# Router fed with the sums ahead of the norm, and the half split of the slab after the experts given to GpSimd

## What is computed

```
proj = x @ w_in[l]                          # retention, window and latent attention follow
mix  = concat([ret_o, swa_o, mla_o]) @ w_out[l]
x    = layer_norm(ALPHA * x + mix, ln1_g[l], ln1_b[l])
scores = sigmoid(x @ router_w)              # 16 experts, one router_w for both layers
biased = scores + router_bias
# best group of 4 (sum of its two best biased scores), then the 2 best experts in it
# gates = their unbiased scores, normalised to sum 1
y    = sum over the chosen experts of down(silu(gate(x)) * up(x) * gate)
x    = layer_norm(ALPHA * x + y, ln2_g[l], ln2_b[l])
```

## Time and profile before

| | us |
|---|---|
| runs, median of 3 | 1554.58 (1554.37 to 1555.19) |
| the profiled execution | 1554.16 |
| its span | 1552.3 |

### The profile page before, as it was taken

One profiled execution on the slowest core, in us unless ns is written; L12 is line 12 of the kernel. 1 busy time (PEld: TensorE's weight loads), 2 busy tenths in 40 slices (PEclk: granted clock), 3 DMA queues, 4 the chain that ended last, 5 costly groups with the idle time before them and its releaser, 6 DMA issues.

```text
span 1552.3 us, 20392 instructions
## 1 busy us (share of the span) xinstructions
PE 1525.1 (98%) x7476; PEld 1167.2 (75%) x7476; DVE 835.7 (54%) x1126; ACT 710.5 (46%) x1179; POOL 88.8 (6%) x159
## 2 busy tenths in 40 slices
PE   8999999999999999999999999999999999999998
PEld 7886445877443788888888888878888888888886
DVE  4675215476422755546667555565555556755544
ACT  5662123674212544446474444453444537554443
POOL 2420000140000000002000000000000010000000
PEclk9999999999999999999999999999999999999999
DMA  7537997546699655566345655546555653655551
GB/s 247 204 135 296 372 421 294 173 142 279 248 421 414 220 184 192 183 207 199 115 156 170 210 191 183 186 152 208 185 185 191 208 164 109 203 190 189 189 189 56
DMA packets 165986, 328.30 MB, mean 211 GB/s; under 512 B 8874, under 2 KB 106896, under 8 KB 152992
## 3 DMA queue, kind: packets, MB, share of 16 engines
q1 hardware_dynamic: 164992, 323.52, 59.5%
q0 software_dynamic: 928, 3.89, 0.8%
HBM read 326.33 MB, written 1.05 MB: 211 GB/s over the span
## 4 chain that ended last, share of the span: by engine, by line
PE 90%; DVE 3%; DMA 3%; ACT 2%; issue 1%; DVEq 1%; POOL 0%; SPq 0%; POOLq 0%; ACTq 0%
PE bank L449 23%; PE bank L451 23%; PE bank L450 23%; PE bank L1221 6%; PE bank L1267 3%; DMA sb_raw<-w_in 2%; PE bank L853 1%; PE bank L1180 1%; PE bank L1181 1%; DMA sb_raw<-ffn_w 1%; PE bank L1275 1%; PE bank L1276 1%; DVE sb_wlo L445 1%; PE bank L930 1%; PE bank L882 1%; ACT sb_whi L438 1%
## 5 line engine op out<-in xcount | busy, mean ns | idle before, releaser
L445 DVE TENSOR_TENSOR sb_wlo<-sb_raw,sb_whi 128x1024 fp32r<-128x1024 f32 (+2 forms) x419 | 483.3, 1197 | 347.4 <-ACT sb_whi L438 347.0
L438 ACT ACTIVATE sb_whi<-sb_raw 128x1024 fp32r<-128x1024 f32 (+2 forms) x419 | 408.0, 1027 | 322.1 <-PE bank L451 303.6
L449 PE MATMUL bank<-sb_whi,sb_op_hi 128*128 128x512 f32 (+2 forms) x1216 | 475.3, 391 | 6.5 <-DVE sb_op_lo L2012 3.5
L451 PE MATMUL bank<-sb_whi,sb_op_lo 128*128 128x512 f32 (+2 forms) x1216 | 467.8, 385 | 0.0
L450 PE MATMUL bank<-sb_wlo,sb_op_hi 128*128 128x512 f32 (+2 forms) x1216 | 467.1, 384 | 0.0
L449 PEld LDWEIGHTS bank<-sb_whi,sb_op_hi 128*128 128x128 f32 x1216 | 228.7, 188 | 53.3 <-issue 4.3
L451 PEld LDWEIGHTS bank<-sb_whi,sb_op_lo 128*128 128x128 f32 x1216 | 228.6, 188 | 46.1
L450 PEld LDWEIGHTS bank<-sb_wlo,sb_op_hi 128*128 128x128 f32 x1216 | 228.9, 188 | 42.6
L449 PE MATMUL bank<-sb_whi,sb_lat_hi 128*128 128x512 f32 (+2 forms) x456 | 175.7, 385 | 1.0 <-DVE sb_wlo L445 1.0
L451 PE MATMUL bank<-sb_whi,sb_lat_lo 128*128 128x512 f32 (+2 forms) x456 | 174.5, 383 | 0.0
L450 PE MATMUL bank<-sb_wlo,sb_lat_hi 128*128 128x512 f32 (+2 forms) x456 | 174.4, 382 | 0.0
(11 more groups left out here) (269 smaller groups left out, 1337.3 us busy)
## 6 DMA issues: line engine op xcount, KB each, us to landing
sb_raw<-ffn_w SPq DMA_DIRECT2D x264, 512.0 KB, 4.3
sb_moe<-exp_w_gate_up SPq DMA_DIRECT2D x46, 1024.0 KB, 9.7
sb_raw<-w_in SPq DMA_DIRECT2D x84, 512.0 KB, 4.6
sb_moe<-exp_w_down SPq DMA_DIRECT2D x26, 1024.0 KB, 10.0
sb_raw<-w_out SPq DMA_DIRECT2D x32, 512.0 KB, 4.4
sb_per_block<-exp_w_gate_up SPq DMA_DIRECT2D x8, 1024.0 KB, 7.0
sb_xT<-exp_w_gate_up SPq DMA_DIRECT2D x6, 1024.0 KB, 10.2
sb_xg<-exp_w_gate_up SPq DMA_DIRECT2D x4, 1024.0 KB, 8.9
```

The costliest lines, as they stand in the source:

```text
L438: nc.scalar.activation(h, r, ACT.Copy).then_inc(hi_made.sem, 1)
L445: nc.vector.tensor_tensor(o, r, h.bitcast(F32), ALU.subtract).then_inc(lo_made.sem, 1)
L449: nc.tensor.matmul(ps, hi, wh, start=first, stop=False)
L451: return nc.tensor.matmul(ps, lo, wh, start=False, stop=last)
```

## The change

There are two parts.

**1. The router is fed with the sums.** The logits of a normed token are ((v − mean)·rstd·g + b)·W, which is rstd · v·W' + b·W, where W' is g·W with its column mean taken off. So the router needs no normed tokens: it takes v, the sums in the banks, and rstd comes in afterwards.

- In layer 0's set-up both layers' W' and b·W are made: GpSimd loads ln1_g and ln1_b beside other vectors (NORM1), VectorE multiplies (4 operations of 128x128) and sums (4 reductions), TensorE adds over partitions by a matmul with ones, 128x64, and VectorE takes off the mean and copies the tails b·W.
- ScalarE copies the four banks to `sums_of` (sums_out, line 1780 of the changed kernel); VectorE's bn_stats wait for these copies. TensorE transposes the sums; chunk 0's eight transposes stand inside the mix, ahead of its last quarter. All copies to xT are on ScalarE.
- VectorE makes the logits from the fold: rstd times it plus the tail (`logits`), and ScalarE's sigmoid reads them.
- The last step of chunk 1's norm goes from VectorE to ScalarE (times rstd, `scaled`) and GpSimd (plus b, two adds of 128x512). Of chunk 0's two token_lo, the second is made by GpSimd (`xs_lo0`), the first stands on VectorE between `hot` and the slot numbers.
- TensorE runs one filler instead of four; open_residual waits for `ln1` and is spread over the stage.

**2. The half split by GpSimd.** The second half of the lo split of the slab that follows the experts is made by GpSimd, between its second and third power −1/2. VectorE's part is the first half, then both last down_lo; at the layer's end it waits until GpSimd has raised `lo_made`.

```diff
@@ GpSimd @@
                 for n in range(4):
+                    if n == 2:
+                        moe_done(pool, l, last_use(WLO_SLOT[1]))
+                        pool.wait_ge(lo_made.sem, 2 * RING + 2 * slab_number(0, S1, l + 1, 1) + 1)
+                        split_lo(pool, slab_number(0, S1, l + 1, 1), 1, parts=(1,), on=nc.gpsimd)
                     pool.wait_ge(F["ln_var"].sem, F["ln_var"].after(l, n + 1))
                     nc.gpsimd.tensor_tensor(lrstd[:, n % 2:n % 2 + 1], lve[:, n % 2:n % 2 + 1], half[:, 0:1], ALU.pow).then_inc(F["ln_rstd"].sem, 1)
+                    if n == 1:
+                        for nh in range(2):
+                            v, cols_of = x[:, 1, 512 * nh:512 * nh + 512], slice(512 * nh, 512 * nh + 512)
+                            pool.wait_ge(F["normed"].sem, F["normed"].after(l, nh + 1))
+                            nc.gpsimd.tensor_tensor(v, v, table[:, 1, cols_of], ALU.add).then_inc(F["ln1"].sem, 1)
+                        pool.wait_ge(F["xs_hi"].sem, F["xs_hi"].after(l, 1))
+                        lo, hi = (t[:, 0, 4:8, :] for t in (xs_lo, xs_hi))
+                        v = x[:, 0, 512:1024].rearrange("p (q j) -> p j q", j=4)
+                        nc.gpsimd.tensor_tensor(lo, v, hi.bitcast(F32), ALU.subtract).then_inc(F["xs_lo0"].sem, 1)
@@ TensorE @@
+                if l == 0:
+                    pe.wait_ge(rw_summed.sem, 1)
+                    nc.tensor.matmul(bank[4][:, 0:2 * DEPTH * NE], c("ones"), rw_sums, start=True, stop=True).then_inc(rw_total.sem, 1)
...
                 for ch in range(NC):
                     for nh in range(2):
                         if ch == 0:
                             slab_ready(num(S1_OUT + 2 + nh))
+                        elif nh == 1:
+                            if l == 0:
+                                pe.wait_ge(rw_centred.sem, 1)
+                            routing_transposes(0)
...
-                routing_transposes(0)
+                routing_transposes(1)
                 router(0)
+                router(1)
+                fold(0)
+                fold(1)
+                wait(F, "ln1", l, 2)
                 open_residual(0)
-                routing_transposes(1)
-                fold(0)
-                router(1)
-                fold(1)
-                open_residual(1)
-                kept_busy(3, 512, const[:, 0:512])
+                wait(F, "ln1", l, 3)
+                open_residual(1, (0,))
+                kept_busy(1, 512, const[:, 0:512])
...
-                kept_busy(1, 512, const[:, 0:512], 7)
+                wait(F, "ln1", l, 4)
+                open_residual(1, (1,))
@@ ScalarE @@
+                sums_out(0, 0)
+                sums_out(0, 1)
+                sums_out(1, 0)
                 routing_out(0)
                 routing_out(1)
+                sums_out(1, 1)
+                routing_out(2)
+                routing_out(3)
                 logit_out(0)
+                logit_out(1)
...
+                wait(F, "scaled", l, 1)
+                scaled(0)
+                wait(F, "logits", l, 1)
+                nc.scalar.activation(scores, biased, ACT.Sigmoid).then_inc(F["routed"].sem, 1)
+                scaled(1)
+                wait(F, "ln1", l, 2)
                 token_hi(0)
-                routing_out(2)
-                logit_out(1)
-                wait(F, "folded", l, 2)
-                nc.scalar.activation(scores.rearrange("p c e -> p (c e)"), bank[5][:, 0:32], ACT.Sigmoid).then_inc(F["routed"].sem, 1)
+                wait(F, "ln1", l, 4)
                 token_hi(1)
@@ VectorE @@
+                def logits():
+                    dve.sem_inc(F["scaled"].sem, 1)
+                    wait(F, "folded", l, 2)
+                    for ch in range(NC):
+                        i = stt(out=biased[:, ch, :], in0=bank[5][:, NE * ch:NE * ch + NE], scalar=lrstd[:, ch:ch + 1],
+                                in1=tails[:, NE * l:NE * l + NE], op0=ALU.mult, op1=ALU.add)
+                    i.then_inc(F["logits"].sem, 1)
...
-                token_lo(0, 0)
-                token_lo(0, 1)
...
+                token_lo(0, 0)
                 wait(F, "ranked", l, 1)
...
+                    following(1, (0,))
                     for nh in range(2):
-                        following(1, (nh,))
                         down_lo(PAIRS - 1, nh)
...
+                dve.wait_ge(lo_made.sem, 2 * RING + 2 * slab_number(0, S1, l + 1, 2))
```

More of the change, by code:

```diff
@@ L396, in program @@
             ("mix_c0", 2, 0), ("ln_var", 4, 0), ("ln_rstd", 4, 0), ("ln1", 4, 0), ("table", 64, 0),
-            ("xT_a", 3, 0), ("xT_d", 1, 0), ("logit", 8, 0), ("logit_out", 2, 0), ("folded", 2, 0), ("routed", 1, 0),
-            ("hot", 1, 0), ("counted", 1, 0), ("ranked", 1, 0), ("sized", 1, 0), ("in_slot", 4, 0), ("xs_hi", 2, 0), ("xs_lo", 4, 0),
+            ("sums_out", 4, 0), ("xT_a", 4, 0), ("logit", 8, 0), ("logit_out", 2, 0), ("folded", 2, 0), ("scaled", 1, 0), ("normed", 2, 0), ("logits", 1, 0), ("routed", 1, 0),
+            ("hot", 1, 0), ("counted", 1, 0), ("ranked", 1, 0), ("sized", 1, 0), ("in_slot", 4, 0), ("xs_hi", 2, 0), ("xs_lo0", 1, 0), ("xs_lo", 3, 0),
             ("gathered", 2 * DK, 0), ("xg_a", 4, 0), ("xg_d", 12, 0), ("gates", 1, 0), ("slot", PAIRS, 0), ("of_slot", PAIRS, 0),
@@ L438, in split_hi, with split_lo @@
                 nc.scalar.activation(h, r, ACT.Copy).then_inc(hi_made.sem, 1)
-        def split_lo(dve, number, slot, first=HALF, second=HALF, parts=(0, 1)):
+        def split_lo(dve, number, slot, first=HALF, second=HALF, parts=(0, 1), on=nc.vector):
             for i, (r, h, o) in enumerate(halves((raw[slot], whi[slot], wlo[slot]), first, second)):
@@ L1183, in early_gather @@
                 def early_gather():
-                    wait(F, "xs_lo", l, 2)
+                    wait(F, "xs_lo0", l, 1)
+                    wait(F, "xs_lo", l, 1)
                     wait(F, "in_slot", l, 1)
@@ L1187, in early_gather @@
                         gather(0, k, gather_bank(k), 0)
-                    wait(F, "xs_lo", l, 3)
+                    wait(F, "xs_lo", l, 2)
                     wait(F, "in_slot", l, 2)
@@ L2180, in _, with layer_norm @@
                 lo1(l, 17)
-                def layer_norm(n0, there, done, between=None):
+                def layer_norm(n0, there, done, between=None, last=None):
                     wait(F, "table", l, 16 * (n0 + 2))
@@ L2200, in layer_norm @@
                         wait(F, "ln_rstd", l, n0 + ch + 1)
+                        if ch and last is not None:
+                            last()
+                            break
                         for nh in range(2):
@@ L2204, in layer_norm @@
                                 op0=ALU.mult, op1=ALU.add).then_inc(F[done].sem, 1)
-                def mixed(ch, nh):
-                    if ch == 0:
-                        wait(F, "mix_c0", l, nh + 1)
-                    else:
-                        slab_is_done(slab_number(0, S1, l, S1_OUT + 2 + nh))
-                layer_norm(0, mixed, "ln1")
+                if l == 0:
+                    dve.wait_ge(rw_total.sem, 1)
+                    for n in range(DEPTH):
+                        stt(out=rw_g[n], in0=bank[4][:, NE * n:NE * n + NE].unsqueeze(1).to_broadcast([P, DK, NE]), scalar=-1.0 / D, in1=rw_g[n],
+                            op0=ALU.mult, op1=ALU.add)
+                    nc.vector.tensor_copy(tails, bank[4][:, DEPTH * NE:2 * DEPTH * NE]).then_inc(rw_centred.sem, 1)
+                def logits():
[5 more added lines that the diff above has]
+                    i.then_inc(F["logits"].sem, 1)
+                layer_norm(0, lambda ch, nh: wait(F, "sums_out", l, 2 * ch + nh + 1), "ln1", last=logits)
                 def token_lo(ch, h):
```

64 lines of the change are left out of this document (44 added, 20 removed).

## The result

The changed kernel takes **1559.53 us** (median of 12 runs, 1557.74 to 1560.72). The kernel before, run beside it, takes 1554.93 us (12 runs, 1554.37 to 1556.2). The ratio is 1.0028, with a 95% interval of 1.002 to 1.0036: the change costs 4.6 us. The forecast was no change, 1554.2 us, with a range up to 1557.6. Near what happened lies only the rival in which TensorE's clock falls, 1558.9 us, and it had a chance of 0.12.

A forecast was written before the change was run, and what follows sets the result against it. TensorE, busy 98% of the span, was taken as the bound, so only its waits and fillers count. Contention net +0.9, ones matmul +0.15 and tail −1.38 summed to −0.33 us: 1554.2 us, range 1548.3 to 1557.6.

The forecast's parts named there:

- the rival in which TensorE's clock falls: Routing stage: TensorE idle from about 135.0 to 138.3 us, clock drops, 1.7 us lost per layer; 1558.9 us, chance 0.12.
- Router ahead of the norm: Routing stage, mix to biased add: feeding the router sums starts the biased add at 132.1 instead of 134.51, 2.4 us gained per layer.
- a start after 133 would refute this step: Sign in the routing stage: a biased add starting after 133 us, instead of near 132.1, disproves the early router's gain.
- GpSimd's hold: Ranking in the routing stage: two adds and xs_lo0 on GpSimd delay VectorE by 2.65 to 3.5 us per layer, taken as 2.85.
- holes ahead of VectorE's operations: Sign in the ranking: 6 us instead of 3.3, with 1 us gaps before two-input operations beside GpSimd's adds.
- The rival without contention: Ranking: GpSimd's operations and VectorE's short ones pass each other; −6.0 us in all, 1548.5 us, chance 0.18.
- the one with half of it: Ranking: one of three overlaps misses or GpSimd delays VectorE by 0.6; cost 1.4 per layer, 1551.3 us, chance 0.10.
- Set-up hidden: Layer 0's start: eight more VectorE operations, +2.2 us, covered by 4.8 us before TensorE uses lat_lo; ones matmul +0.15.
- half split −1.38: End of the experts: GpSimd's split removes TensorE's waits for xs_lo, 0.52 and 0.86 us, so −1.38 us.
- The sum: Whole kernel: +0.9 +0.15 −1.38 = −0.33 us, giving 1554.2 us, no measurable change.
- my own case: Whole kernel: early router offset by GpSimd delaying VectorE, plus the tail gain; 1554.2 us, span 1553.5 to 1555.7, chance 0.52.
- the experts wait for no weights: Expert stretch: DMA queues at 0.00 from 148 to 155 us, so any gain or loss at the gather passes on whole.

The follow-up runs named there:

- the changed kernel with fillers: The changed kernel with five fillers on TensorE ahead of the wait for hot instead of one: 1556.25 us against 1556.15 for the kernel before, ratio 1.0.
- the half split alone: The kernel before with only the change's second part, GpSimd's lo split after the experts: 1554.27 us against 1555.95, ratio 0.9989.
- the second profile of the kernel before: The kernel before, unchanged, profiled once more for its start: attention's first product at 62.20 us, 0.75 later than in its first profile.
- the run with shrunk adds: The changed kernel with GpSimd adding b to 8 columns of each half of chunk 1 and making xs_lo0 only after hot: 1552.62 us, ratio 0.9977.
- the router alone: The changed kernel with the lo split after the experts back on VectorE: 1561.98 us against 1556.15 for the kernel before, ratio 1.0038.

## Why the prediction was wrong

- **Router ahead of the norm, 2.4 us gained for each layer: right.** From the end of the mix to the biased add it was 7.6 us before (126.91 to 134.51) and is 4.36 after (129.46 to 133.82), less the eight transposes, whose pace is 0.79, and the ones matmul: 2.3 us. The biased add started at 133.82, and I had written that a start after 133 would refute this step. By the letter it does; but the changed kernel's profile is 1.4 us late from its start on, and without that the add is at 132.4.
- **GpSimd's hold, 2.65 to 3.5 us, taken as 2.85: right.** Measured 3.1 and 3.0 in the changed kernel's two layers. The duration worked out from the slope, 1.27 us, is what the adds take (2.51 for two); the strided xs_lo0 takes 1.54. Only the picture was off: I had looked for holes ahead of VectorE's operations, and the time is inside their records. The rival without contention (0.18) and the one with half of it (0.10) are out.
- **Set-up hidden, half split −1.38: right.** The stretch from TensorE's first wait at 30 us to the attention is not longer after than before (31.65 to 62.86 against 30.18 to 61.45), so the set-up on VectorE costs nothing that shows. The tails gained 0.8 and 0.7 us in the profile, and the half split alone 1.7 in the medians.
- **The sum was right, and the kernel it describes is the changed kernel with fillers**: 1556.25 against 1556.15, where I had worked out −0.33; the interval is 1.4 us to either side. Two slips in it changed nothing. The span of my own case, 1553.5 to 1555.7, mixes two bases: from 1554.25 its terms give 1553.9 to 1556.2. And that the experts wait for no weights was read from seven microseconds, 148 to 155. Later profiles have such waits near the experts' end, 0.42 us in the second profile of the kernel before and 0.79 with the half split alone, so a gain there isn't always passed on whole.
- **The step that failed is the one that gave TensorE's fall of clock 0.12**, and with it left the edit of the fillers at a price of nothing. I had the place of the hole and nearly its length (135.0 to 138.3; it was 137.06 to 140.45, of which 1.4 is the late start), and its price in both layers, 3.4 us (measured 1.1 + 2.6 = 3.7). What I set against it, that TensorE is busy up to the hole, turned out to be no argument: a hole of 2.1 us behind busy openings was enough in the kernel before, and two of 0.7 us each in layer 1 of the run with shrunk adds. The trace of before could not show a fall there, because its fillers prevented one. The Trainium skill's "TensorE: Matmul & The Clock Gate", Part 1, which calls the slow state the default that activity releases, was the sentence to weigh more. By it the fillers are part of the path. The trace agrees: without them the kernel before falls to a granted clock of 0.50 and takes 1.7 us more.
- The range ended at 1557.6, which held this mechanism only on top of my own sum. What was measured, 1559.53, lies 1.9 above. I haven't split that up: the hold was 0.2 us longer in each layer than my term, the clock cost 0.3 more, and the base itself moves. The kernel before, whose 1554.58 I had built on, took 1554.93 us beside it and 1555.84 to 1556.15 in the later sets.

## What to carry to other kernels

Before work goes to GpSimd, look at what VectorE does at that moment. If it has instructions with two inputs in SBUF, a short step lasts until GpSimd's instruction ends, and a chain of them pays once for each of GpSimd's. Price the removal of fillers as if the clock falls (here it fell after holes of 3.4 and 2.1 us, and once after two of 0.7), and try the kernel with the fillers kept before the idea behind the change is judged. Here the same idea cost 4.6 us with GpSimd beside the ranking and without fillers, and gained 5.2 us with VectorE's own waits used instead.

## What the runs showed of the hardware

- One input on GpSimd's side is enough for the hold: a copy of 512 columns (0.64 us) held a two-input VectorE operation of 0.18 us to 0.56. The Trainium skill's "SBUF — State Buffer", section "Who interferes with whom", says that a VectorE instruction with two SBUF inputs contends with a GpSimd instruction that reads SBUF; the trace agrees with that wording. The section also says that a VectorE instruction with at most one SBUF input doesn't contend, outside modes with two ports that no run here is known to use; the trace agrees (0.25 us for the reduction, beside GpSimd and not, and 0.69 against 0.68 for down_lo).
- The hold goes to whoever begins first, both ways: in the run with shrunk adds GpSimd's xs_lo0 waited out VectorE's token_lo (2.18 us instead of 1.54), and VectorE's in_slot then waited for it (1.22 instead of 0.69).
- The same clock fall cost 1.1 us in layer 0 and 2.6 in layer 1 of one execution: in layer 1 it had begun before the counts, which took 0.59 us a row instead of 0.37, in layer 0 only behind them. Which layer pays more isn't fixed: in the router alone, with the same routing stage, the counts took 0.59 us in layer 0, and the two stages were 3.5 and 2.0 us longer than before instead of 2.0 and 3.15.
- The time to the first attention product varied from 61.45 to 63.34 us among the profiles, with no relation that shows to what the kernels do in that stretch.
